# Gate and up projections as seven products of half blocks instead of eight

## The chip, the cores and the metric

The kernel runs on the 8 cores of one Trainium2 chip. Each core takes 2048 of the 16384 tokens (4 batches of 4096) and all of the weights; the cores do not talk to each other. The metric is the device time of the slowest core, in microseconds.

## What is computed

One layer of a hybrid block, of which the second half changes here:

```python
merged = (sigmoid(g_a) * y_a + sigmoid(g_p) * y_p + sigmoid(g_x) * y_x)
x = x + merged @ w_out[l]
# ---- SwiGLU channel mixer ----
h = rms_norm(x, norm_ffn[l])
x = x + (silu(h @ w_gate[l]) * (h @ w_up[l])) @ w_down[l]
return rms_norm(x, norm_final)
```

The model width is 1024 and the width of the channel mixer 2816. Matmuls take bf16 and sum in f32. The branches y_a (a short gated convolution), y_p (pooling over 2, 4, 8 and 16 positions) and y_x (attention to 256 memory tokens) come before.

## The kernel before

A core treats its tokens as two halves of 1024. Activations lie transposed, channels on partitions: `HA` holds the normed input of a half, 8 blocks of 128 channels (kc) by 1024 tokens. Weights come through a ring of 12 slots of 128 x 2048 bf16; a load reads f32 from memory, is issued from GpSimd's queue (`slot_load`, L218) and waits until the slot's readers are done and until the load eight issues back has landed. PSUM has 8 banks of 512 f32 columns, handed out in turn. All matmuls are recorded at L228. The class `Plan` writes one program for each engine: each engine runs its instructions in the order in which the Python code emits them, and a wait is set wherever an operand was written or read elsewhere.

Order of the work: mixer of half 0, merge of half 0, then `conv_units` of half 1, `merge(1, ...)` in 8 chunks of six units of 16 matmuls (`merge_chunk`: the products for gate a at L451 and L454, the pooling sums at L460 to L492, the merged block at L494), then `ffn(0)` and `ffn(1)`. `s_hook` is called at three places of each merge chunk, place 2 being in front of the last unit.

`ffn(hf)` has 22 chunks (NF) and a down stage. A chunk c has one slot with 128 columns of w_gate and 128 of w_up for all 1024 channels. `gu_g` multiplies the gate part (16 matmuls of 512 columns into two banks) and ScalarE's Silu puts it into `T[c % 2]` (L625). `gu_u` multiplies the up part, and VectorE multiplies by the Silu into `actT` (L629). Slot loads run four chunks ahead. In half 0 the first four chunks also have the output projection of half 1, two tiles of 16 matmuls each (`o1`, sum at L585), whose weights are the four `sO` slots; and in 11 of the chunks (WD) a piece of w_down is loaded (L955). The down stage has 8 tiles of 128 tokens, 44 matmuls each; per tile come the sum (L994), square (L1011), root (L325), reciprocal (L327), scaling (L331) and the store. The down stage of half 0 also norms the input tiles of half 1 and transposes them into `HA` (`Norm`, `c_trans`, by DMA on SP's queue); three of the eight norms are begun in chunks 14 to 18. `T` are seven f32 buffers of 1044 columns.

Of the kernel before, what the change touches and what calls it, by code (L numbers as in the profile page):

```python
# [85 lines left out]
def build_program():  # L86
# [36 lines left out]
    def kA(a0, n=1):  # L123
        return [("A", a) for a in range(a0, a0 + n)]
# [498 lines left out]
    def gu_g(c, s):
        u = Unit(lambda kc: rg(s, kc * P, (kc + 1) * P), s, (H0.rhs, H0.keys)).run()
        act(lambda e: e.activation(out=T[c % 2][:, 0:TM], in_=u.ps(), func=AF.Silu), u.keys(), [("T", c % 2)])  # L625

    def gu_u(c, s):
        u = Unit(lambda kc: rg(s, 1024 + kc * P, 1024 + (kc + 1) * P), s, (H0.rhs, H0.keys)).run()
        dve(lambda e: e.tensor_tensor(out=actT[:, c, :], in0=u.ps(), in1=T[c % 2][:, 0:TM], op=ALU.mult),  # L629
            u.keys() + [("T", c % 2)], kA(c))  # L630
# [229 lines left out]
    for j in range(4, 8):  # L860
# [82 lines left out]
    WD = (4, 5, 6, 8, 9, 10, 12, 13, 14, 16, 17)  # L943
    LASTB = ((0, 512), (512, 256), (768, 256))

    def ffn(hf):
        gu = [slot_load(w_gu_d[c]) for c in range(4)]
        cp, cq = [], []
        for c in range(NF):
            if c + 4 < NF:  # L950
                gu.append(slot_load(w_gu_d[c + 4]))
            if hf == 0 and c in WD:
                q = 2 * WD.index(c)
                dst = atoms(NF + q, 2)
# [12 lines left out]
        if hf == 0:
            cq.append(x1_load(1, 3))
            nxt = [3, 4]
        ydq = [x1_load(hf, 0)]  # L970
        for i in range(NT):
            b = banks(2)

            def grp(kcs, nbs=(0, 1)):
                return [(bank(b + nb), actT[:, kc, i * P:(i + 1) * P], wdT[:, kc, nb * 512:(nb + 1) * 512],
                         kc == 0, kc == NF - 1) for nb in nbs for kc in kcs]
            last = hf == 1 and i == NT - 1
            if i == 0:
# [17 lines left out]
            if hf == 0:
                for _ in range(2 if i in (2, 3) else 1):
                    if cp:
                        c_trans(*cp.pop(0))
                    if cq:  # L1000
                        q2 = cq.pop(0)
                        cp.append((Norm(T[q2][:, 0:D], [("T", q2)]).finish(), nxt[0]))
                        nxt[0] += 1
                    if nxt[1] < NT:
                        cq.append(x1_load(1, nxt[1]))
                        nxt[1] += 1
# [142 lines left out]
```

How the kernel before makes its waits and increments, by code:

```python
        def f(eng):  # L1064
            for waits, fn, semkey, inc in plan.ops[ename]:
                for sk, v in waits:
                    eng.wait_ge(sems[sk], v)
                ins = fn(eng)
                ins.then_inc(sems[semkey], inc)
```

## Time and profile before

| | us |
|---|---|
| median of 3 runs | 1153.46 |
| lowest and highest | 1153.25, 1158.1 |
| the profiled execution, its own time | 1155.09 |
| its span, slowest core (core 0) | 1153.5 |
| spans of the other cores | 1144.2 to 1151.8 |

The profile is of one execution, on the slowest core. Busy time is the time in which an engine's records run; matmuls overlap, so their mean duration (379 ns) is more than the distance between two of them. The last column of a group or of a timeline names what ended the idle time in front of an instruction. The granted clock is the share of full speed that TensorE had.

### The profile page before, as it was taken

The numbers are of one execution on the slowest core, as the hardware profiler recorded it, in microseconds if no ns is written. First come the engines' busy times: TensorE is split into PE (matmuls) and PEld (weight loads), VectorE is DVE, ScalarE is ACT, GpSimd is POOL, SyncE is SP. The second block draws the span as 40 slices with busy tenths as digits, with TensorE's granted clock in tenths as the row PEclk, the third lists the DMA queues.
The fourth block names the chain that finished last, engine by engine and source line by source line (L and its number), as shares of the span: only waits on it lengthen the run. The fifth ranks groups of instructions, "written<-read, shape, count | busy, mean of one in ns | idle before, by whom it ended". The sixth has DMA issues, their size and how long they took to land.

```text
span 1153.5 us, 14599 instructions; the slowest of 8 cores (1144.2 to 1153.5 us)
## 1 busy us (share of the span) xinstructions
PE 1117.5 (97%) x5472; PEld 543.1 (47%) x5574; DVE 475.7 (41%) x482; ACT 305.2 (26%) x490; POOL 79.0 (7%) x153
## 2 busy tenths in 40 slices
PE   7998999997999999999999999999999999999998
PEld 3665545553444444444444444444444444444444
DVE  5452555462765654654554632111324221112223
ACT  5432443423212224331212210111522121111111
POOL 1110000100011010001001000211000000000000
PEclk9998999999999999999999999999999999999999
DMA  9999861478387979345226453999966354200132
GB/s 246 173 205 203 148 128 55 80 159 127 74 137 209 258 164 175 67 123 110 56 54 110 74 146 110 204 182 171 172 164 194 101 117 82 40 1 1 37 110 110
DMA packets 78916, 146.34 MB, mean 127 GB/s; under 512 B 46571, under 2 KB 46571, under 8 KB 78592
## 3 DMA queue, kind: packets, MB, share of 16 engines
q0 software_dynamic: 21456, 77.64, 39.6%
q1 hardware_dynamic: 57392, 67.78, 20.2%
q8 instruction: 45, 0.74, 0.3%
q14 instruction: 23, 0.19, 0.1%
HBM read 185.27 MB, written 23.07 MB: 181 GB/s over the span
## 4 chain that ended last, share of the span: by engine, by line
PE 85%; DMA 10%; DVE 2%; issue 2%; ACT 1%; SPq 0%; DVEq 0%; ACTq 0%; POOLq 0%
PE ps L228 85%; DMA ring<-w_in 3%; DMA ring<-w_kv 3%; DMA arena<-hb 3%; DMA arena<-x 1%; ACT tmp L419 1%; DVE tmp L390 0%; SPq L177 0%; DVE tmp L470 0%; DVE smx L416 0%; DVE tmp L383 0%; DVE arena L397 0%; ACT tmp L387 0%; DVE tmp L483 0%; DVE hb L331 0%
## 5 line engine op out<-in xcount | busy, mean ns | idle before, releaser
L228 PE MATMUL ps<-hA,ring 128*128 128x512 bf16 (+3 forms) x2446 | 503.5, 363 | 6.6 <-ACT hA L352 2.5
L228 PEld LDWEIGHTS ps<-hA,ring 128*128 128x128 bf16 x2496 | 243.2, 98 | 259.6 <-issue 5.2
L228 PE MATMUL ps<-arena,ring 128*128 128x512 bf16 (+1 forms) x1575 | 333.3, 369 | 13.1 <-ACT tmp L460 6.1
L228 PEld LDWEIGHTS ps<-arena,ring 128*128 128x128 bf16 x1600 | 158.0, 99 | 184.2 <-issue 14.7
L228 PE MATMUL ps<-arena 128*128 128x512 bf16 (+1 forms) x838 | 180.4, 373 | 0.8
L629 DVE TENSOR_TENSOR arena<-ps,tmp 128x1024 bf16<-128x1024 f32 x44 | 53.9, 1225 | 227.9 <-PE ps L228 224.1
L228 PEld LDWEIGHTS ps<-arena 128*128 128x128 bf16 x854 | 83.6, 98 | 96.3
L625 ACT ACTIVATE tmp<-ps 128x1024 f32<-128x1024 f32 x44 | 45.0, 1023 | 253.4 <-PE ps L228 253.4
L470 DVE TENSOR_TENSOR tmp<-tmp 128x1024 f32<-128x1024 f32 (+6 forms) x40 | 49.2, 1230 | 41.4 <-ACT tmp L460 38.9
L228 PE MATMUL ps<-ring,arena 128*128 128x512 bf16 x250 | 57.4, 379 | 0.6 <-issue 0.2
L218 POOL DMA_DIRECT2D ring<-w_in x48 | 25.6, 538 | 440.0 <-PE ps L228 359.3
L994 DVE TENSOR_TENSOR tmp<-ps,tmp 128x1024 f32<-128x1024 f32 x15 | 18.4, 1224 | 79.6 <-PE ps L228 79.6
L390 DVE SCALAR_TENSOR_TENSOR tmp<-tmp,smallc 128x1024 f32<-128x1024 f32 x32 | 41.1, 1284 | 21.8 <-ACT tmp L387 20.1
L419 ACT ACTIVATE tmp<-ps,smx 128x256 f32<-128x256 f32 x64 | 30.3, 473 | 69.0 <-DVE smx L416 58.1
L454 DVE TENSOR_TENSOR tmp<-ps,tmp 128x1024 f32<-128x1024 f32 x16 | 19.6, 1224 | 64.6 <-PE ps L228 63.9
L1011 ACT ACTIVATE tmp<-tmp 128x1024 f32<-128x1024 f32 x15 | 15.8, 1056 | 114.2 <-DVE tmp L994 92.6
L218 POOL DMA_DIRECT2D ring<-w_gate_up x44 | 23.3, 531 | 324.1 <-PE ps L228 277.3
L228 PEld LDWEIGHTS ps<-ring,arena 128*128 128x128 bf16 x256 | 24.9, 98 | 30.7 <-issue 1.0
L383 DVE TENSOR_TENSOR tmp<-ps,tmp 128x1044 f32<-128x1044 f32 (+1 forms) x16 | 19.7, 1234 | 43.4 <-PE ps L228 43.4
L460 ACT ACTIVATE tmp<-ps 128x1044 f32<-128x1044 f32 (+1 forms) x16 | 16.5, 1030 | 77.2 <-PE ps L228 76.9
L451 ACT ACTIVATE tmp<-ps 128x1024 f32<-128x1024 f32 x16 | 16.4, 1024 | 76.9 <-PE ps L228 76.8
L585 DVE TENSOR_TENSOR arena<-ps,arena 128x1024 f32<-128x1024 f32 x16 | 19.6, 1222 | 38.1 <-PE ps L228 38.1
(98 smaller groups left out, 583.6 us busy)
## 6 DMA issues: line engine op xcount, KB each, us to landing
ring<-w_in POOLq DMA_DIRECT2D x48, 512.0 KB, 12.9
ring<-w_gate_up POOLq DMA_DIRECT2D x44, 512.0 KB, 12.2
arena<-x SPq DMA_DIRECT2D x32, 512.0 KB, 6.7
tmp<-x_scr SPq DMA_DIRECT2D x24, 512.0 KB, 5.3
x_scr<-arena SPq DMA_DIRECT2D x16, 512.0 KB, 3.5
out<-tmp SPq DMA_DIRECT2D x15, 512.0 KB, 3.3
arena<-w_down POOLq DMA_DIRECT2D x11, 512.0 KB, 24.3
ring<-w_kv POOLq DMA_DIRECT2D x8, 512.0 KB, 23.1
```

Source lines behind the costliest of these rows:

```text
L218: plan.op("pool", lambda e: e.dma_start(out=dst, in_=src), reads=list(reads), writes=[s.key()], dma=True)
L228: ins = e.matmul(o, l, r, start=s0, stop=s1)
L383: dve(lambda e: e.tensor_tensor(out=like(pp[:, lo:TH], u), in0=u.ps(), in1=like(ca[:, lo:TH], u), op=ALU.mult), u.keys() + [("T", tb)], [( ...
L390: dve(lambda e, k=k: e.scalar_tensor_tensor(out=cv[:, 0:TM], in0=pp[:, HALO - 2 + k:HALO - 2 + k + TM], scalar=cw(j, k), in1=cv[:, 0:TM], ...
L419: act(lambda e, h=h: e.activation(out=ex[:, h * 256:(h + 1) * 256], in_=PS[:, b * 512 + h * 256:b * 512 + (h + 1) * 256], func=AF.Exp, bia ...
L454: dve(lambda e, u=u: e.tensor_tensor(out=mm_[:, 0:TM], in0=u.ps(), in1=sa[:, 0:TM], op=ALU.mult), u.keys() + [("T", 0)], [("T", 3)])
L460: act(lambda e, u=u: e.activation(out=like(up[:, (0 if u.halo else HALO):TH], u), in_=u.ps(), func=AF.Copy), u.keys(), [("T", 4)])
L470: dve(lambda e, dst=dst, src=src, lo=lo, k=k: e.tensor_tensor(out=dst[:, lo:TH], in0=src[:, lo:TH], in1=src[:, lo - k:TH - k], op=ALU.add) ...
L585: dve(lambda e: e.tensor_tensor(out=xb(q), in0=bank(b, 2), in1=xb(q), op=ALU.add), kB(b, 2) + kX(q), kX(q))
L625: act(lambda e: e.activation(out=T[c % 2][:, 0:TM], in_=u.ps(), func=AF.Silu), u.keys(), [("T", c % 2)])
L629: dve(lambda e: e.tensor_tensor(out=actT[:, c, :], in0=u.ps(), in1=T[c % 2][:, 0:TM], op=ALU.mult), u.keys() + [("T", c % 2)], kA(c))
L994: dve(lambda e, b=b, y=y: e.tensor_tensor(out=y, in0=bank(b, 2), in1=y, op=ALU.add), kB(b, 2) + [("T", q)], [("T", q)])
```

## The change

- Gate and up of a chunk become a product of 2 x 2 blocks: rows gate and up (128 columns of weights each), inner halves channels 0 to 511 and 512 to 1023, columns tokens 0 to 511 and 512 to 1023. Strassen's scheme in Winograd's form takes seven products of half blocks, each 4 matmuls of 512 columns, for the eight of before.
- Sums of activations (`x_sums`): three new blocks held in three ring slots through the whole of `ffn`, and two blocks of `HA` overwritten by differences; 5 VectorE instructions for each of four pairs of token tiles. For half 0 they are made in merge chunks 4 and 5 of half 1, for half 1 in the down stage.
- Sums of weights (`w_sums`), one chunk ahead: one of 1024 columns on VectorE (here called W), one of 512 (A) and a difference of 1024 that rewrites the middle of the slot (S) on GpSimd. W and A go to the memory of `kT` and `vT`. S waits for W, as W reads what S overwrites; the first product of a chunk waits for S.
- Three PSUM banks a chunk; ScalarE copies four products out and does two Silus; VectorE does five sums of 512 columns in f32 and the final product, now from SBUF. `T[0]` is shared by all chunks, three more buffers alternate between even and odd chunks.
- Loads: slot c + 4 is requested behind chunk c and no longer ahead of it; the first two gate and up slots of half 0 are requested in merge chunk 6. The weight sums of chunk 0 are emitted at place 2 of merge chunk 7, and on GpSimd's queue that is ahead of the four loads of w_out.
- All eight norms of half 1 lie in the down stage of half 0, two a tile in tiles 1 to 4, in the order 0, 4, 1, 5, 2, 6, 3, 7.

```diff
     def slot_new():
+        while st["slot"] % RING in slots_held:
+            st["slot"] += 1
         s = Ref("S", st["slot"] % RING)
...
+    def x_slots():
+        for n in ("11+22", "21+22", "11+12"):
+            xq[n] = slot_new()
+            slots_held.add(xq[n].key()[1])
+
+    def x_sums(p):
+        x11, x12, x21, x22 = x_view(0, 0, p), x_view(0, 1, p), x_view(1, 0, p), x_view(1, 1, p)
+        lo, hi = [("HA", p + 1)], [("HA", p + 5)]
+
+        def dst(n):
+            return ring[:, xq[n].key()[1], :].rearrange("p (k t) -> p k t", k=4)[:, :, p * P:(p + 1) * P]
+
+        def tt(o, i0, i1, op, rd, wr):
+            dve(lambda e: e.tensor_tensor(out=o, in0=i0, in1=i1, op=op), rd, wr)
+        tt(dst("11+22"), x11, x22, ALU.add, lo + hi, [xq["11+22"].key()])
+        tt(dst("11+12"), x11, x12, ALU.add, lo, [xq["11+12"].key()])
+        tt(dst("21+22"), x21, x22, ALU.add, hi, [xq["21+22"].key()])
+        tt(x12, x12, x22, ALU.subtract, lo + hi, lo)
+        tt(x21, x21, x11, ALU.subtract, lo + hi, hi)
+
+    wx = [kT[:, :, :].rearrange("p k t -> p (k t)"), vT[:, :, :].rearrange("p k t -> p (k t)")]
+    wxk = [[("kT",)], [("vT",)]]
+
+    def w_sums(c, s):
+        e_, ek = wx[c % 2], wxk[c % 2]
+        sk = [s.key()]
+        w = rg(s, 0, SW)
+        pairs = w.rearrange("p (a b) -> p a b", a=2)
+        w11, w22 = rg(s, 0, 512), rg(s, 1536, 2048)
+        ends = w.rearrange("p (a b) -> p a b", a=4)[:, 0:4:3, :]
+        mid = rg(s, 512, 1536)
+        dve(lambda e: e.tensor_tensor(out=e_[:, 0:1024], in0=pairs[:, 0, :], in1=pairs[:, 1, :], op=ALU.add), sk, ek)
+        plan.op("pool", lambda e: e.tensor_tensor(out=e_[:, 1024:1536], in0=w11, in1=w22, op=ALU.add),
+                reads=sk, writes=[("wA", c % 2)])
+        plan.op("pool", lambda e: e.tensor_tensor(out=mid.rearrange("p (a b) -> p a b", a=2),
+                                                  in0=mid.rearrange("p (a b) -> p a b", a=2), in1=ends, op=ALU.subtract),
+                reads=sk + ek, writes=sk)
+
+    def gate_up(c, s, Q):
+        e_, ek, wa = wx[c % 2], wxk[c % 2], [("wA", c % 2)]
+        q4, q3, q1, q2 = Q
+        k4, k3, k1, k2 = [[("T", q)] for q in Q]
+        T4, T3, T1, T2 = [T[q] for q in Q]
+        lo, hi = [("HA", t) for t in range(1, 5)], [("HA", t) for t in range(5, 9)]
+        bD, bA, bC = banks(1), banks(1), banks(1)
+
...
+        L, R = slice(0, 512), slice(512, 1024)
+        prod(bD, ws_(1536), xs_("11+12"), True)
+        cp(T4[:, R], bD, [("q5", q4)] + k4)
+        prod(bA, we(1024, wa), xs_("11+22"), True)
+        cp(T3[:, L], bA, k3)
+        prod(bC, ws_(512), xh(1, 1), True)
+        cp(T4[:, L], bC, k4)
+        tt(T3[:, R], T4[:, L], T4[:, R], ALU.subtract, k4, [("qt", q3)])
+        prod(bD, ws_(1024), xh(0, 0), False)
+        cp(T1[:, L], bD, k1)
+        tt(T3[:, L], T3[:, L], T3[:, R], ALU.add, k3 + [("qt", q3)], k3)
+        prod(bA, we(512, ek), xh(0, 1), False)
+        tt(T2[:, L], bank(bA), T3[:, R], ALU.add, kB(bA, 1) + [("qt", q3)], k2)
+        prod(bC, ws_(0), xs_("21+22"), False)
+        cp(T2[:, R], bC, [("q2r", q2)], AF.Silu)
+        act(lambda e: e.activation(out=T2[:, L], in_=T2[:, L], func=AF.Silu), k2, k2)
+        tt(T3[:, L], T3[:, L], bank(bC), ALU.subtract, k3 + kB(bC, 1) + [("q2r", q2)], k3)
+        prod(bD, we(0, ek), xh(1, 0), False)
+        tt(T1[:, R], T3[:, L], bank(bD), ALU.add, k3 + kB(bD, 1), k1)
+        tt(actT[:, c, :], T1[:, 0:TM], T2[:, 0:TM], ALU.mult, k1 + k2 + [("q2r", q2)], kA(c))
 
 
...
     def s_hook(j, pos):
         s_tail()
+        if j in (4, 5) and pos == 2:
+            if j == 4:
+                x_slots()
+            x_sums(2 * (j - 4))
+            x_sums(2 * (j - 4) + 1)
+        if j == 6 and pos == 0:
+            gu0.extend(slot_load(w_gu_d[c]) for c in range(2))
+        if j == 7 and pos == 2:
+            w_sums(0, gu0[0])
 
...
     def ffn(hf):
-        gu = [slot_load(w_gu_d[c]) for c in range(4)]
-        cp, cq = [], []
+        gu = list(gu0)
+        while len(gu) < 4:
+            gu.append(slot_load(w_gu_d[len(gu)]))
+        gu0.clear()
         for c in range(NF):
-            if c + 4 < NF:
-                gu.append(slot_load(w_gu_d[c + 4]))
+            if c + 1 < NF:
+                w_sums(c + 1, gu[c + 1])
             if hf == 0 and c in WD:
                 q = 2 * WD.index(c)
                 dst = atoms(NF + q, 2)
                 plan.op("pool", lambda e, dst=dst, q=q: e.dma_start(out=dst, in_=w_down_d[:, q * D:(q + 2) * D]),
                         writes=kA(NF + q, 2), dma=True)
-            gu_g(c, gu[c])
+            r = roles[hf]
+            gate_up(c, gu[c], (r[0], r[1 + 3 * (c % 2)], r[2 + 3 * (c % 2)], r[3 + 3 * (c % 2)]))
             o1(hf, 2 * c)
-            gu_u(c, gu[c])
             o1(hf, 2 * c + 1)
-            if hf == 0 and NF - 8 <= c < NF - 5:
-                cq.append(x1_load(1, c - NF + 8))
-            if hf == 0 and NF - 6 <= c < NF - 3:
-                q = cq.pop(0)
-                n_ = Norm(T[q][:, 0:D], [("T", q)])
-                cp.append((n_.finish(), c - NF + 6))
+            if c + 4 < NF:
+                gu.append(slot_load(w_gu_d[c + 4]))
+        cq, cp, cx = [], [], []
+        ydq = [x1_load(hf, 0)]
         if hf == 0:
-            cq.append(x1_load(1, 3))
-            nxt = [3, 4]
-        ydq = [x1_load(hf, 0)]
+            cq = [(x1_load(1, t), t) for t in CO[0:2]]
         for i in range(NT):
             b = banks(2)
+            if hf == 0:
+                for p in cx:
+                    x_sums(p)
+                cx = []
+                for b_, t in cp:
+                    c_trans(b_, t)
+                    if t >= 4:
+                        cx.append(t - 4)
+                cp = []
+                if 1 <= i <= 4:
+                    for q2, t in cq:
+                        cp.append((Norm(T[q2][:, 0:D], [("T", q2)]).finish(), t))
+                    cq = [(x1_load(1, t), t) for t in CO[2 * i:2 * i + 2]]
+                if i == 1:
+                    gu0.extend(slot_load(w_gu_d[c]) for c in range(4))
+                if i == NT - 1:
+                    w_sums(0, gu0[0])
 
...
```

## Rows read from the trace of the kernel before

**Rows 1.** The page: busy us of each engine, share of the span, instructions.

```profile
PE 1117.5 (97%) x5472; PEld 543.1 (47%) x5574; DVE 475.7 (41%) x482; ACT 305.2 (26%) x490; POOL 79.0 (7%) x153
```

**Rows 2.** Busy time by stretch: from:to, length, engines, PEclk, DMA share, GB/s.

```profile
720.00:843.00 123.00, 122.42 (x560) 55.74 (x570) 26.23 (x24) 30.90 (x36) 19.01 (x36) 1.00 1.00 179
...
920.00:1071.00 151.00, 150.26 (x688) 68.41 (x700) 28.38 (x24) 25.15 (x26) 5.28 (x10) 1.00 0.24 46
```

**Rows 3.** Timeline of half 1's chunks: start, length, engine, line, operation.

```profile
982.39 1.23 DVE L629 TENSOR_TENSOR arena<-ps,tmp 128x1024 bf16<-128x1024 f32 x1 [5.68 <-PE ps L228]
...
985.76 1.02 ACT L625 ACTIVATE tmp<-ps 128x1024 f32<-128x1024 f32 x1 [5.49 <-PE ps L228]
...
996.20 1.23 DVE L629 TENSOR_TENSOR arena<-ps,tmp 128x1024 bf16<-128x1024 f32 x1 [5.68 <-PE ps L228]
```

**Rows 4.** Timeline of the last tile and of VectorE at 642: lengths and gaps.

```profile
1143.33 0.69 DVE L1022 TENSOR_TENSOR tmp<-ps,tmp 128x512 f32<-128x512 f32 x1 [0.27 <-PE ps L228]
1144.12 0.63 ACT L1025 ACTIVATE tmp<-tmp 128x512 f32<-128x512 f32 x1 [2.70 <-DVE tmp L1022]
1144.13 0.69 DVE L1029 TENSOR_TENSOR tmp<-tmp,gB 128x512 f32<-128x512 f32 x1
...
642.73 1.22 DVE L486 TENSOR_TENSOR tmp<-tmp 128x1024 f32<-128x1024 f32 x1
643.96 1.22 DVE L492 TENSOR_TENSOR tmp<-ps,tmp 128x1024 f32<-128x1024 f32 x1
```

**Rows 5.** Groups of the whole span, shapes apart: count, busy us, mean ns.

```profile
L486 DVE TENSOR_TENSOR tmp<-tmp 128x1024 f32<-128x1024 f32 x16 | 19.6, 1225 | 1.7
...
L350 DVE COPY hA<-ps 128x1024 bf16<-128x1024 bf16 x4 | 2.7, 685 | 0.9 <-PE ps L343 0.9
```

**Rows 6.** Timeline from merge chunk 7 into chunk 0 of half 0.

```profile
650.80 1.22 DVE L454 TENSOR_TENSOR tmp<-ps,tmp 128x1024 f32<-128x1024 f32 x1 [4.29 <-PE ps L228]
...
663.52 1.23 DVE L486 TENSOR_TENSOR tmp<-tmp 128x1024 f32<-128x1024 f32 x1
664.34 3.62 PE L228 MATMUL ps<-hA,ring 128*128 128x512 bf16 x16
...
665.11 0.53 POOL L218 DMA_DIRECT2D ring<-w_gate_up  x1 [2.93 <-PE ps L228]
...
671.59 1.23 DVE L585 TENSOR_TENSOR arena<-ps,arena 128x1024 f32<-128x1024 f32 x1 [4.38 <-PE ps L228]
```

**Rows 7.** Timeline from down tile 7 of half 0 into half 1.

```profile
919.89 9.44 PE L228 MATMUL ps<-hA,ring 128*128 128x512 bf16 x42
920.23 1.22 DVE L994 TENSOR_TENSOR tmp<-ps,tmp 128x1024 f32<-128x1024 f32 x1 [5.15 <-PE ps L228]
...
922.79 0.20 ACT L325 ACTIVATE stat<-stat 128x1 f32<-128x1 f32 x1
...
924.73 0.33 SPq L177 DMA_DIRECT2D out<-tmp  x1
```

**Rows 8.** Loads of w_out for half 1: first issue of 4, and landing.

```profile
606.40 0.53 POOL L218 DMA_DIRECT2D ring<-w_out  x1 [23.70 <-PE ps L228]
...
DMA to landing us min/median/max: 5.7/6.3/7.1
```

**Rows 9.** GpSimd's timeline with loads queued: first and last of 12 issues.

```profile
769.57 0.53 POOL L218 DMA_DIRECT2D ring<-w_gate_up  x1 [3.08 <-DVE arena L629]
...
802.25 0.53 POOL L218 DMA_DIRECT2D ring<-w_gate_up  x1 [2.62 <-DMA ring<-w_gate_up]
```

**Rows 10.** A wait of TensorE in merge of half 0: timeline, then PE by stretch.

```profile
287.16 5.08 PE L228 MATMUL ps<-arena,ring 128*128 128x512 bf16 x16 [6.12 <-ACT tmp L460]
...
288.00:290.00 2.00, 2.00 (x6) 0.50 0.00 0
```

**Rows 11.** VectorE's scaling in a down tile of half 0.

```profile
894.80 1.28 DVE L331 SCALAR_TENSOR_TENSOR tmp<-tmp,stat,gB 128x1024 f32<-128x1024 f32 x1
```

**Rows 12.** The page: transfers, KB each, median us from issue to landing.

```profile
out<-tmp SPq DMA_DIRECT2D x15, 512.0 KB, 3.3
```

More of the change, by code:

```diff
@@ L167, in build_program @@
     st = {"slot": 0, "pb": 0, "stat": 0, "hb": 0, "sm": 0}
-    held = set()
+    held, slots_held = set(), set()
     def act(fn, reads, writes):
@@ L621, in c_trans @@
         dma_transpose(b, HA[:, :, TOK0 + i * P:TOK0 + (i + 1) * P], [("HA", i + 1)])
[L623 to L630, printed above, removed]
+    xq = {}
@@ new lines, in x_view @@
+    def x_view(tk, kh, p):
+        t0 = TOK0 + tk * 512 + p * P
+        return HA[:, kh * 4:(kh + 1) * 4, t0:t0 + P]
+    def x_slots():
[14 more added lines that the diff above has]
+        tt(x21, x21, x11, ALU.subtract, lo + hi, hi)
@@ new lines, in gate_up, with xs_, xh, ws_ @@
+    def gate_up(c, s, Q):
[5 more added lines that the diff above has]
+        bD, bA, bC = banks(1), banks(1), banks(1)
+        def xs_(n):
+            return (lambda k: ring[:, xq[n].key()[1], k * 512:(k + 1) * 512]), [xq[n].key()]
+        def xh(tk, kh):
+            return (lambda k: HA[:, kh * 4 + k, TOK0 + tk * 512:TOK0 + (tk + 1) * 512]), (hi if tk else lo)
+        def ws_(o):
+            return (lambda k: rg(s, o + k * P, o + (k + 1) * P)), [s.key()]
+        def we(o, keys):
+            return (lambda k: e_[:, o + k * P:o + (k + 1) * P]), keys
+        def prod(b, w, x, first):
+            mms = [(bank(b), w[0](k), x[0](k), first and k == 0, k == 3) for k in range(4)]
+            def fn(e):
+                ins = None
+                for (o, l, r, s0, s1) in mms:
+                    ins = e.matmul(o, l, r, start=s0, stop=s1, skip_group_check=True)
+                return ins
+            plan.op("pe", fn, reads=w[1] + x[1], writes=kB(b, 1))
+        def cp(o, b, wr, fn=AF.Copy):
+            act(lambda e: e.activation(out=o, in_=bank(b), func=fn), kB(b, 1), wr)
+        def tt(o, i0, i1, op, rd, wr):
+            dve(lambda e: e.tensor_tensor(out=o, in0=i0, in1=i1, op=op), rd, wr)
+        L, R = slice(0, 512), slice(512, 1024)
[18 more added lines that the diff above has]
+        tt(actT[:, c, :], T1[:, 0:TM], T2[:, 0:TM], ALU.mult, k1 + k2 + [("q2r", q2)], kA(c))
@@ L871, in build_program @@
         conv_units(0, H0, j, cs[j // 2], [f0, None, (lambda k=k: s_step(H0, k + 1))])
+    gu0 = []
     def s_hook(j, pos):
         s_tail()
+        if j in (4, 5) and pos == 2:
[7 more added lines that the diff above has]
+            w_sums(0, gu0[0])
     def merge(hf, H, first):
@@ L924, in build_program @@
     TB = [2, 3, 4, 5, 6]
+    roles = [[0, 1, 2, 3, 4, 5, 6], [0, 1, 2, 3, 4, 5, 6]]
     tn = {"n": 0}
@@ L944, in build_program @@
     LASTB = ((0, 512), (512, 256), (768, 256))
+    CO = (0, 4, 1, 5, 2, 6, 3, 7)
     def ffn(hf):
-        gu = [slot_load(w_gu_d[c]) for c in range(4)]
-        cp, cq = [], []
+        gu = list(gu0)
+        while len(gu) < 4:
+            gu.append(slot_load(w_gu_d[len(gu)]))
+        gu0.clear()
         for c in range(NF):
-            if c + 4 < NF:
-                gu.append(slot_load(w_gu_d[c + 4]))
+            if c + 1 < NF:
+                w_sums(c + 1, gu[c + 1])
             if hf == 0 and c in WD:
@@ L995, in ffn @@
                 kB(b, 2) + [("T", q)], [("T", q)])
[L996 to L1006, printed above, removed]
             if i + 1 < NT:
```

## The prediction

> **What bounds the kernel now.** I read the page first, then the stretches, then single chunks of the stage that changes. TensorE is busy 97% of the span [rows 1]. By stretches, most gate and up chunks of half 0 (720 to 843 us) and those of half 1 (920 to 1071) keep it over 99% busy at a granted clock of 1.00 [rows 2]. So an instruction counts there only if it is a matmul or makes one wait. In half 1 one chunk follows another every 6.91 us: VectorE's multiplies start at 982.39 and, two chunks on, 996.20 [rows 3]. A chunk is 32 matmuls of 512 columns, so one takes 6.907/32 = 0.2158 us (the 379 ns of the records overlap). In that chunk VectorE works 1.23 us and ScalarE 1.02 us; GpSimd only issues transfers.
>
> **What is removed.** A chunk has 28 matmuls in place of 32: 6.04 us, 0.863 less. Over 44 chunks that is 38.0 us, if TensorE stays the bound.
>
> **VectorE's new work in a chunk.** Five sums of 512 f32 columns (subtract for T3 right, add for T3 left, T2 left, subtract for T3 left, T1 right) at 0.69 each [rows 4]; the product, both inputs now in SBUF, 1.225 (the SBUF-only sum of L486 costs what the PSUM one does) [rows 5]; the weight sum W of 1024 bf16 columns. For W there is no row of a bf16 pair in SBUF: the bf16 copy of 1024 columns takes 0.685, the f32 sum 1.225 [rows 5]. I take 0.69, the row with its type, and keep 1.225 for the range. Total 5 x 0.69 + 1.225 + 0.69 = 5.37. Between instructions stand 0.11 us where one needs the last one's result and about 0.02 otherwise (642.73 + 1.22 to 643.96) [rows 4]; three of the first kind and four of the second: 0.41. VectorE's round is 5.78 us of 6.04. ScalarE: four copies and two Silus of 512, each about 0.6 (half of 1.02 and some start; a 512 square is 0.63 [rows 4]), 3.6 us: no bound.
>
> **GpSimd's new work.** It gets A, a sum of 512 bf16 columns, and S, a difference of 1024. No row shows it computing: its 153 instructions are issues of 0.53 us [rows 1, 6]. Lower bound of S: VectorE's 1.225. Upper bound: the two inputs fetched one after the other, twice that, 2.45. A start of 0.16 plus 0.533 for each 512 columns fits VectorE's rows (0.69 and 1.225); with two passes but one start, S is 0.16 + 4 x 0.533 = 2.29 and A 1.23. I take these, near the upper end, as GpSimd's 0.53 for merely handing over a transfer speaks for no faster engine. The Trainium skill (GPSIMD Engine Reference, Elementwise side-by-side) has a two-input sum of 2048 columns at 4497 ns on GpSimd, so about 2.25 for 1024; by it the sum below would move by under 2 us.
>
> **The new chain.** W(c+2) stands on VectorE behind the product of chunk c; S(c+2) waits for W(c+2); all of chunk c+2 on TensorE waits for S(c+2), since S rewrites the slot. Let chunk c start at 0 and count 0.3 from the end of matmuls to the next engine (the last one starts at 919.89, VectorE at 920.23 [rows 7]). Third product ends 2.59, its copy about 3.5, T3 right can start at 3.6. The sixth ends 5.18, its Silu about 6.1; T3 left's subtraction 6.2 to 6.9, T1 right to 7.7, product 7.8 to 9.0, W to 9.7, S 9.8 to 12.1. Chunk c+2 is due at 12.08. So even with both engines free to work at once this comes out level: some 6.10 us a chunk.
>
> **Do GpSimd and VectorE work at once?** This decides the case, and the trace of before cannot say, because GpSimd never computes in it. Of VectorE's seven instructions four have both inputs in SBUF (W, T3 right, T3's addition, the product: 3.30 us), three read PSUM. Ends: nothing is lost, or S stands wholly in VectorE's round. Right behind W come T3 right and T3's addition, both with two SBUF inputs, so S, which may start when W ends, falls just on these. If they exclude each other the round is 5.78 + 2.29 = 8.07; A, which comes behind S and a 0.53 issue, then falls on the PSUM readers and costs nothing. I take this end: a sum of two SBUF tensors is the one kind of work both would do, and no row supports counting on overlap. The Trainium skill (SBUF — State Buffer, Who interferes with whom) says that the two engines share one SBUF port pair, held by whichever comes first for its whole instruction, also against a VectorE instruction with two SBUF inputs if GpSimd reads SBUF. By that rule the chunk is the 8.07; without it 6.10. It speaks against this change.
>
> In chunks 0 to 3 of half 0 the output projection adds two tiles of 16 matmuls, 6.91 us, and only 2 x 1.23 to VectorE [rows 6]: TensorE, at 12.95, stays the bound over 8.07 + 2.46 = 10.5 there. These give 4 x 0.863 = 3.5 back. Of the other 40, about 39.5 are paced by VectorE (one starts from an idle engine): 39.5 x (8.07 - 6.907) = 45.9 lost.
>
> **Entry to half 0.** W(0) stands in VectorE's queue behind all pool sums of merge chunk 7: L486 ends at 664.75 [rows 6], W(0) near 665.5, S(0) from 665.6 to 667.9. TensorE would start chunk 0 at 664.34 and now starts at 668.0: 3.6 lost. Behind S(0) on GpSimd stand the four w_out loads, which before went out from 606.40 on [rows 8]; nothing hides that move. Each landed after 5.7 to 7.1 us, median 6.3 [rows 8]; when loads are queued one comes through about every 3.0 us (12 issues, 11 steps, between 769.57 and 802.25, most of them held for an earlier load [rows 9]). The last lands at 668.0 + 6.3 + 3 x 3.0 = 683.3. The first output tile is due at 668.0 + 6.04 = 674.0: 9.3 lost, bounds 3 and 12. Behind a stall of 6.1 us at 281 to 287 the granted clock was 0.50 (1.2 GHz) and 16 matmuls took 5.08 instead of 3.45 us [rows 10]: 1.6 more. The two early gate_up loads and the three held slots cost nothing: merge chunk 7's slots come free one merge chunk before they are used.
>
> **Sums of activations.** 20 VectorE instructions of 512 bf16 columns a half, 0.43 to 0.69 each. In merge chunks 4 and 5, 10 each, under 7 us: of six units of 3.45 us VectorE idles 4.29 us in one stretch alone [rows 6] and PSUM holds three further units. In the down stage VectorE does a sum, a short reciprocal and a scaling a tile now, 1.22 + 1.28 and some 0.2 [rows 7, 11]; two norms (2.9) and five sums (at most 3.5) make 9.0 of 9.5 us, and the last sums are a tile ahead. The moved norms leave the chunks, where VectorE has no room. The four SP transfers more a tile fit in 9.5 us. Cost 0; if one came late, chunk 0 of half 1 would wait for it.
>
> **Entry to half 1.** Down tile 7's square and root hold ScalarE until 3.1 us behind the end of the matmuls (919.89 to 922.99 [rows 7]); the copy that frees the first bank then ends at 3.7, 1.2 late. The fourth product's copy goes to buffer 2, which holds tile 7's output: store issued at 924.73, landing 3.3 later [rows 7, 12], so 8.1 behind the matmuls; the copy and TensorE's seventh product follow at 9.1 in place of 5.2: 3.9 lost. At the end of each half the last product is 3 to 6 us behind TensorE; the first down tile has 40 matmuls, 8.6 us, before it: 0.
>
> **Sum.** 1153.5 - 3.5 + 45.9 + 3.6 + 9.3 + 1.6 + 3.9 = 1214.3 of span. The profiled execution took 1155.1 with a span of 1153.5; the median of the three runs is 1153.46, so I carry the +60.8 over to it: 1214.
>
> **Rivals.**
> (1) The engines overlap freely. A chunk is 6.10: 44 x (6.91 - 6.10) = 35.5 gained, 18.4 lost at the two entries: 1136. It decides wherever S does not hold VectorE back; the change wins if S and T3 right run at once. For it: three of seven instructions read PSUM, and nothing in the trace shows a collision. If W takes 1.225 besides, VectorE's round is 6.32: 44 x 0.59 = 25.8 gained, 18.4 lost, 1146, at the edge of what can be told from no change.
> (2) They exclude each other, but VectorE wins the short gap before T3's addition, and S runs beside the PSUM readers. The sums that exclude each other make 3.30 + 2.29 + 1.23 = 6.8, with handovers 7.0: 1153.5 + 39.5 x 0.1 - 3.5 + 18.4 = 1172. Against it: S has waited since the end of W and the gap is 0.11 us.
> (3) The 2 us for which TensorE waits in each chunk bring the clock to 1.2 GHz, or S costs above 2.45: beyond 1240. Against it: before, the clock was down only behind waits of 6 us [rows 10].
> (4) The change doesn't do what it says, 32 matmuls' worth of time remains: excluded by the count of products, 7 x 4.
>
> **How the numbers follow.** Forecast 0.45 (1196 to 1240: S at 1.7 to 2.45, W up to 1.225, entries of 10 to 21). Rival 1 0.24 with W fast, 0.06 with W slow (half of that faster, half the same). Rival 2 and what lies between it and the forecast 0.15. Rival 3 0.07. What I have not seen, on the fast side, 0.03. Both signs hold much, so the range reaches from rival 1's 1136 less 6 for cheaper entries to the forecast's upper end: 1130 to 1240; the forecast alone is 1196 to 1240. A measurement of this kernel tells 0.5%, 5.8 us, from no change. Faster 0.24 + 0.03 + 0.03 = 0.30, same 0.03, slower 0.45 + 0.15 + 0.07 = 0.67.
>
> **What would show it.** The forecast: chunks spaced near 8.1 us, VectorE over 70% busy with gaps or long instructions where S runs, TensorE waiting for GpSimd's difference. Rival 1: chunks near 6.1, S beside T3 right with neither longer. Entries: TensorE idle 3.6 us at 664, then 9 us before the first output tile with ring<-w_out as releaser, and near 4 us in chunk 0 of half 1 behind ScalarE's copy. I am wrong above all if S neither lengthens nor delays its neighbours on VectorE.

## The result, and the profile after

| | before | after |
|---|---|---|
| median of 4 runs | 1155.78 us | 1178.57 us |
| ratio, with its 95% interval | 1 | 1.0191 [1.015, 1.0231] |
| the profiled execution | 1155.09 us | 1176.2 us |
| its span, slowest core | 1153.5 us (core 0) | 1174.7 us (core 6) |
| spans of all cores | 1144.2 to 1153.5 | 1163.6 to 1174.7 |

The change makes the kernel 1.9% slower. Slower was the likelier side of the forecast, but by 61 us; it is 23. In some executions, whatever the kernel, the cores of one die run at a lower granted clock and take longer (one of the four after, 1251.77 us); the two medians of the table hold such executions, the ratios and all later times do not. The page of the kernel after, its first section, and its waits between 660 and 1100 us (who waited for whom: us in total, times, longest):

```profile
PE 1104.1 (94%) x5398; PEld 526.3 (45%) x5398; DVE 732.5 (62%) x786; ACT 402.7 (34%) x704; POOL 235.8 (20%) x241
```

```profile
PE ps L696 <- POOL ring L666: 37.0, 37, 3.3
...
PE ps L230 <- DMA ring<-w_out: 9.1, 1, 9.1
...
PE ps L696 <- ACT tmp L701: 4.5, 3, 2.2
```

Against [rows 1] VectorE (DVE) has 257 us more and GpSimd (POOL) 157; TensorE waits 37 times for S, GpSimd's difference at L666, 1 us each on average. (Of the matmuls of before some records are missing, 5472 against 5574 weight loads; the weight loads, now 5398, are fewer by the full 176, four a chunk.) The groups of the chunks, shapes apart, between 700 and 1100 us:

```profile
L704 DVE TENSOR_TENSOR tmp<-tmp 128x512 f32<-128x512 f32 x84 | 127.3, 1515 | 7.7 <-ACT tmp L701 3.4
...
L666 POOL TENSOR_TENSOR ring<-ring 128x1024 bf16<-128x1024 bf16 x41 | 97.4, 2375 | 205.6 <-DVE kT L663 135.8 <-DVE vT L663 69.8
...
L704 DVE TENSOR_TENSOR tmp<-tmp,ps 128x512 f32<-128x512 f32 x84 | 57.1, 680 | 8.6 <-DVE tmp L704 4.5 <-PE ps L696 2.6
```

Two kinds of VectorE sum of the same shape stand here. Those with one input in PSUM take 680 ns, as in [rows 4]. Those with both in SBUF, the on-chip memory that holds the slots, the activations and `T` (they are T3 right and T3's addition, from here on the pair), take 1515 on average, and the timeline of half 1 shows which:

```profile
996.85 1.23 DVE L704 TENSOR_TENSOR arena<-tmp 128x1024 bf16<-128x1024 f32 x1
...
997.99 0.68 DVE L663 TENSOR_TENSOR vT<-ring 128x1024 bf16<-128x1024 bf16 x1
...
998.59 3.21 DVE L704 TENSOR_TENSOR tmp<-tmp 128x512 f32<-128x512 f32 x2
...
998.88 2.38 POOL L666 TENSOR_TENSOR ring<-ring 128x1024 bf16<-128x1024 bf16 x1 [3.04 <-DVE vT L663]
...
1001.40 1.02 PE L696 MATMUL ps<-ring 128*128 128x512 bf16 x4 [0.91 <-POOL ring L666]
1001.72 0.68 DVE L704 TENSOR_TENSOR tmp<-ps,tmp 128x512 f32<-128x512 f32 x1
1001.79 1.17 POOL L664 TENSOR_TENSOR kT<-ring 128x512 bf16<-128x512 bf16 x1
```

Behind W (L663) the pair takes 3.21 us; S runs at the same time and ends at 1001.26, and only then does the pair end, at 1001.80. In the last chunk of half 1, where no S follows, the same pair takes 1.48:

```profile
1090.41 1.48 DVE L704 TENSOR_TENSOR tmp<-tmp 128x512 f32<-128x512 f32 x2
1091.81 0.68 DVE L704 TENSOR_TENSOR tmp<-ps,tmp 128x512 f32<-128x512 f32 x1
```

The products of chunks 0 and 20 of half 1 start at 946.97 and 1089.27: 7.115 us a chunk, where [rows 3] give 6.907 and 28 matmuls need 6.04. One round of VectorE, from start to start in the rows above and their neighbours, is 3.13 (pair) + 0.60 + 0.84 + 0.80 (the three that read PSUM) + 1.14 (product) + 0.60 (W) = 7.11: the round fills the chunk.

**Where the 21 us of span come from**, by TensorE's first matmul of each stage:

| stage | before | after | difference |
|---|---|---|---|
| merge ends, half 1 | 664.34 | 658.4 | -5.9 (another core) |
| chunks 0 to 3 of half 0 | 55.3 | 69.3 | +14.0 |
| chunks 4 to 21 of half 0 | 124.3 | 128.0 | +3.7 |
| down, half 0 | 76.0 | 78.9 | +2.9 (granted clock 0.96) |
| chunks of half 1 | 151.95 | 158.1 | +6.1 |
| down, half 1, to the end | 81.7 | 81.95 | +0.3 |

So the larger part comes from the entry to half 0 and not from the steady chunks. The first row is no gain: core 0 of before came late to this point (its cores 1 to 3 at 655 to 656), cores 0 to 3 of after come to it at 654 to 657. The 2.9 of the down stage are the clock of cores 4 to 7 alone: on cores 0, 1 and 3 of the same execution, with the same norms in it and a clock of 1.00, the stage takes 76.0 as before.

That entry, in the timeline, answers to [rows 6]:

```profile
658.54 0.69 DVE L663 TENSOR_TENSOR kT<-ring 128x1024 bf16<-128x1024 bf16 x1
...
659.14 1.22 DVE L494 TENSOR_TENSOR tmp<-ps,tmp 128x1024 f32<-128x1024 f32 x1
659.37 2.12 POOL L666 TENSOR_TENSOR ring<-ring 128x1024 bf16<-128x1024 bf16 x1 [41.46 <-DVE kT L663]
660.46 2.11 DVE L496 TENSOR_TENSOR arena<-tmp 128x1024 bf16<-128x1024 f32 x1
661.43 2.16 POOL L220 DMA_DIRECT2D ring<-w_out  x4
661.75 1.27 PE L696 MATMUL ps<-ring 128*128 128x512 bf16 x4 [3.35 <-POOL ring L666]
...
678.77 9.07 PE L230 MATMUL ps<-ring,arena 128*128 128x512 bf16 x32 [9.13 <-DMA ring<-w_out]
```

TensorE waits 3.35 us for S(0) and 9.13 for w_out, whose loads GpSimd issues only behind S(0), at 661.43 and so some 55 us later than before [rows 8]. After that the two output tiles take 8.91 us, from 678.77 to the next product at 687.68, instead of 6.91, with the clock down (TensorE's clock is the column before the last two):

```profile
662.00:669.00 7.00, 7.00 (x26) 0.76 0.69 109
669.00:679.00 10.00, 0.87 (x4) 0.68 1.02 154
679.00:688.00 9.00, 9.00 (x34) 0.79 0.99 207
688.00:700.00 12.00, 12.00 (x52) 0.90 0.71 178
```

On this core the mean clock stayed at 1.00 only from 700 us on. The waits explain only a part of that. Core 1 of the same execution waited as long (3.35 and 9.82 us) and had its full clock back by 688:

```profile
679.00:688.00 9.00, 9.00 (x33) 0.76 0.86 182
688.00:700.00 12.00, 12.00 (x57) 1.00 0.72 197
```

So had cores 0, 2 and 3. Cores 4 to 7 had 1.00 from 685 to 690 and then 0.81 to 0.84 from 690 to 696, with TensorE busy all the time.

The entry also shows one S beside both kinds of instruction. L494 of the kernel after, with one input in PSUM, runs beside S(0) and takes 1.22 us. L496, with two in SBUF, starts before S(0) ends at 661.49 and takes 2.11; in the kernel before the same instruction stands at L494 and took 1.23:

```profile
665.98 1.23 DVE L494 TENSOR_TENSOR arena<-tmp 128x1024 bf16<-128x1024 f32 x1
```

### The profile page after: what moved, and what is told of

Read it like the earlier page. It is cut to its first block, busy times and chain, and to the rows that moved or that the text cites. A ratio compares the mean times of both kernels' runs of the same rounds, so it can differ in the third digit from the quotient of the medians.

```text
span 1174.7 us, 15935 instructions; the slowest of 8 cores (1163.6 to 1174.7 us)
## 1 busy us (share of the span) xinstructions
PE 1104.1 (94%) x5398; PEld 526.3 (45%) x5398; DVE 732.5 (62%) x786; ACT 402.7 (34%) x704; POOL 235.8 (20%) x241
## 4 chain that ended last, share of the span: by engine, by line
PE 72%; DMA 9%; POOL 7%; DVE 4%; issue 3%; ACT 3%; SPq 0%; POOLq 0%; ACTq 0%; DVEq 0%
PE ps L230 61%; PE ps L696 11%; POOL ring L666 7%; DMA ring<-w_in 3%; DMA ring<-w_q_t 2%; ACT tmp L701 2%; DMA arena<-x 1%; DMA ring<-w_out 1%; DMA ring<-w_kv 1%; DVE kT L663 1%; DVE vT L663 1%; ACT tmp L421 1%; DVE tmp L392 0%; SPq L177 0%; DVE smx L418 0%
## 5 line engine op out<-in xcount | busy, mean ns | idle before, releaser
L230 PE MATMUL ps<-hA,ring 128*128 128x512 bf16 (+4 forms) x1088 | 205.4, 347 | 5.6 <-ACT hA L354 2.6
L701 ACT ACTIVATE tmp<-ps 128x512 f32<-128x512 f32 x220 | 126.2, 592 | 117.6 <-PE ps L696 104.8
L666 POOL TENSOR_TENSOR ring<-ring 128x1024 bf16<-128x1024 bf16 x44 | 103.7, 2358 | 253.9 <-DVE kT L663 183.9
L230 PEld LDWEIGHTS ps<-hA,ring 128*128 128x128 bf16 x1088 | 106.5, 98 | 98.2 <-issue 13.7
L704 DVE TENSOR_TENSOR tmp<-tmp 128x512 f32<-128x512 f32 x88 | 132.6, 1507 | 13.3 <-ACT tmp L701 8.7
L696 PE MATMUL ps<-ring 128*128 128x512 bf16 x352 | 90.7, 380 | 37.0 <-POOL ring L666 37.0
L696 PE MATMUL ps<-hA,ring 128*128 128x512 bf16 x352 | 84.4, 382 | 2.3 <-ACT tmp L701 2.3
L696 PEld LDWEIGHTS ps<-ring 128*128 128x128 bf16 x352 | 31.8, 97 | 87.2 <-issue 54.8
L704 DVE TENSOR_TENSOR tmp<-tmp,ps 128x512 f32<-128x512 f32 x88 | 59.9, 680 | 9.6 <-DVE tmp L704 4.7
L704 DVE TENSOR_TENSOR arena<-tmp 128x1024 bf16<-128x1024 f32 x44 | 54.4, 1237 | 5.7 <-DVE tmp L704 2.8
L1117 DVE TENSOR_TENSOR tmp<-ps,tmp 128x1024 f32<-128x1024 f32 x15 | 18.4, 1224 | 59.5 <-PE ps L230 59.5
L696 PEld LDWEIGHTS ps<-hA,ring 128*128 128x128 bf16 x352 | 34.6, 99 | 45.2 <-issue 5.1
```

The costliest lines, as they stand in the source:

```text
L230: ins = e.matmul(o, l, r, start=s0, stop=s1)
L666: plan.op("pool", lambda e: e.tensor_tensor(out=mid.rearrange("p (a b) -> p a b", a=2), in0=mid.rearrange("p (a b) -> p a b", a=2), in1=en ...
L696: ins = e.matmul(o, l, r, start=s0, stop=s1, skip_group_check=True)
L701: act(lambda e: e.activation(out=o, in_=bank(b), func=fn), kB(b, 1), wr)
L704: dve(lambda e: e.tensor_tensor(out=o, in0=i0, in1=i1, op=op), rd, wr)
```

## The experiments

The theory to test: S on GpSimd and a VectorE instruction with both inputs in SBUF exclude each other. The rivals: VectorE is simply full (load), or TensorE waits at the end of the chain W, S, first product (latency). Chunk spacings are those of the products in chunks 4 to 20 of half 0, or of as many as the text says.

**All sums on VectorE.** In `w_sums`:

```diff
-        plan.op("pool", lambda e: e.tensor_tensor(out=e_[:, 1024:1536], ...   # A
+        plan.op("dve", lambda e: e.tensor_tensor(out=e_[:, 1024:1536], ...
-        plan.op("pool", lambda e: e.tensor_tensor(out=mid..., op=ALU.subtract), ...   # S
+        plan.op("dve", lambda e: e.tensor_tensor(out=mid..., op=ALU.subtract), ...
```

> A and S, the weight sums of GpSimd, go to VectorE; everything else as in the changed kernel. Exclusion theory (in the changed kernel S and VectorE's instructions with two SBUF inputs take turns; of the 7.11 us of a chunk 5.38 are VectorE's own and 1.73 the turns): VectorE's round becomes 5.38 + 0.35 (A) + 0.60 (S) = 6.33 us, T3's addition takes 0.69 again instead of 2.4, the chunk is 6.3; and as no sum stands on GpSimd's queue ahead of the w_out loads, their wait of 9 us goes. 1178.6 - 39.5 x 0.78 - 13 = about 1135. Load theory (VectorE is simply full, its long sums are long by themselves): two more instructions make the chunk 7.11 + 0.95 = 8.06, about 1200. Latency theory (the chain W, S, TensorE bounds): S at 0.6 instead of 2.1 shortens the chain, the chunk falls to 6.04, about 1123.

Measured: 1132.2 us, ratio to before 0.9793 [0.9713, 0.9874], the span of the profiled execution 1130.6. The chunk is 6.54 us (718.04 to 822.61, 16 steps). More work on VectorE made it faster: the load theory is out. The latency theory wanted 6.04, but a full VectorE could hide that here, so it is tested separately below. The pair is back at 1.48 and S takes 0.69:

```profile
981.69 0.69 DVE L666 TENSOR_TENSOR ring<-ring 128x1024 bf16<-128x1024 bf16 x1
...
982.30 1.48 DVE L704 TENSOR_TENSOR tmp<-tmp 128x512 f32<-128x512 f32 x2
```

The chunk is 0.2 above the 6.33 expected: W, A and S take 0.60, 0.52 and 0.61 from start to start, 1.73 together where I had counted 1.55.

**A and S left out.**

```diff
-        plan.op("pool", ...)   # A and S, both
-        prod(bA, we(1024, wa), xs_("11+22"), True)
+        prod(bA, we(512, ek), xs_("11+22"), True)
```

> A and S are left out (two of the seven products use wrong weights), all waits on them with them; W and the rest stay. Exclusion theory: VectorE's round is its own 5.38, TensorE bounds with 28 matmuls, chunk 6.04, 1178.6 - 39.5 x 1.07 - 13 = about 1123. Load theory: the chunk stays near 7.1 and the time near 1165. Latency theory: 6.04, as exclusion. The pair of 512-column f32 sums behind W takes 1.4 and not 3.2 us by the exclusion and latency theories.

Measured: 1114.3 us (one run), chunk 6.04 (715.92 to 812.54, 16 steps), the pair 1.48. The load theory falls here again; exclusion and latency are not told apart.

**Nobody waits for S.**

```diff
-        plan.op("pool", ... out=mid..., in0=mid..., in1=ends, op=ALU.subtract), reads=sk + ek, writes=sk)
+        plan.op("pool", ... out=hb[3]..., in0=mid..., in1=ends, op=ALU.subtract), reads=sk + ek, writes=[("hb", 3)])
```

> S runs on GpSimd at the same moment with the same inputs, behind W, but writes to a spare buffer: no instruction of TensorE waits for it (the half blocks that S should make stay as loaded, so two products have wrong weights). Exclusion theory: VectorE is held up as before, the chunk stays 7.1 though nobody waits for S, and S stays 2.4 long; the time changes only by the 3.4 us wait of chunk 0: about 1175. Latency theory: with TensorE free of S the chunk is 6.04 to 6.1, about 1135.

Measured: 1170.33 us (one run), chunk 7.13 (735.49 to 849.58, 16 steps).

```profile
985.28 3.21 DVE L704 TENSOR_TENSOR tmp<-tmp 128x512 f32<-128x512 f32 x2
985.51 2.44 POOL L666 TENSOR_TENSOR hb<-ring 128x1024 bf16<-128x1024 bf16 x1 [2.90 <-DVE kT L663]
```

TensorE now waits for nothing of S. In the chunks it waits for copies (37.6 us in 39 waits): ScalarE's Silu waits for a sum of VectorE (97.0 us in 41 waits), and the copies stand behind it in ScalarE's queue. The chunk is as long as in the kernel after. The wait for w_out is still there and longer, 14.7 us, as chunk 0 now starts at once (655.88) while the loads still go out behind S (659.16). The latency theory is out: S costs by standing in VectorE's way, not by its own length in the chain.

**S beside the PSUM readers.** W and S two chunks ahead with a third buffer, emitted behind T3's addition; A on VectorE; the entries mended as in the next but one:

```diff
+            if c % 3 == 2: return hb[3][:, a:b] if b <= 1024 else hb[2][:, a - 1024:b - 1024]
...
         tt(T3[:, L], T3[:, L], T3[:, R], ALU.add, k3 + [("qt", q3)], k3)
+        if nxt is not None:
+            w_sums(c + 2, nxt)
```

> With both entries mended, S stays on GpSimd with its full 2.1 us, but W and S are made two chunks ahead (third buffer in hb) and emitted behind T3's addition, so S runs beside T2 left, T3 left's subtraction and T1 right, which read PSUM; A goes to VectorE. Exclusion theory: none of the three gets longer than 0.69, S stays near 2.12 and VectorE's round is 5.38 + 0.35 = 5.73: chunk 6.04 to 6.15, about 1112. Rival (it is GpSimd's sum as such that slows VectorE): the three PSUM readers get longer by some 1.7 us together and the chunk stays near 7.1 to 7.4, about 1155.

Measured: 1114.5 us, ratio to before 0.9694 [0.964, 0.9747]. The chunk is 6.00 (726.25 to 822.26, 16 steps, chunks 5 to 21), in which VectorE makes up a delay; TensorE's chunks 4 to 21 take 6.05 each (711.67 to 820.66).

```profile
990.40 1.33 DVE L712 TENSOR_TENSOR arena<-tmp 128x1024 bf16<-128x1024 f32 x1
...
993.33 0.68 DVE L671 TENSOR_TENSOR hb<-ring 128x1024 bf16<-128x1024 bf16 x1
...
993.93 0.42 DVE L672 TENSOR_TENSOR hb<-ring 128x512 bf16<-128x512 bf16 x1
994.27 0.68 DVE L712 TENSOR_TENSOR tmp<-ps,tmp 128x512 f32<-128x512 f32 x1
994.51 2.12 POOL L674 TENSOR_TENSOR ring<-ring 128x1024 bf16<-128x1024 bf16 x1 [3.33 <-DVE hb L672]
...
994.87 1.47 DVE L712 TENSOR_TENSOR tmp<-tmp,ps 128x512 f32<-128x512 f32 x2
```

S still takes its 2.12 us on GpSimd, in the same kernel and every chunk, but beside instructions that read PSUM; none of them gets longer (0.68, and 1.47 for two), and S is 2.12 instead of 2.38. Where S's end still meets the product, which has two SBUF inputs, the product takes up to 1.33 instead of 1.23 (the row at 990.40; the S of that chunk runs from 988.52 to 990.64). This carries the verdict: it is not GpSimd's sum as such, it is what VectorE reads meanwhile. With all sums made it is the fastest kernel of the case, 3.1% faster than before, though 3.15 us of the wait for w_out are left in it.

**A copy, and a memset, in the place of S.** Both from the kernel in which nobody waits for S:

```diff
-        plan.op("pool", lambda e: e.tensor_tensor(out=hb[3]..., in0=mid..., in1=ends, op=ALU.subtract), ...
+        plan.op("pool", lambda e: e.tensor_copy(out=hb[3][:, :], in_=mid), ...      # the one
+        plan.op("pool", lambda e: e.memset(hb[3][:, :], 0.5), ...                   # the other
```

> As the kernel in which nobody waits for S, but S is a copy of 1024 columns with one input instead of a difference with two (its result goes to a spare buffer, the half blocks S should make stay as loaded). Exclusion theory: a copy reads SBUF too, so T3's addition waits for it; if it takes half of S, 1.1 us, the pair T3 right and T3's addition takes about 3.2 - 1.0 = 2.2 and the chunk is 7.11 - 1.0 = 6.1, about 1135. Rival (only a second input of GpSimd collides): the pair takes 1.48, chunk 6.04.

> As before, but S is a memset of 1024 columns, which reads nothing (the half blocks S should make stay as loaded). If only reads of SBUF exclude each other, the pair T3 right and T3's addition takes 1.48 us whatever the memset's length, and the chunk is 6.04. If any use of SBUF by GpSimd excludes VectorE's instructions with two SBUF inputs, the pair is longer by the memset's length less some 0.4.

Measured: 1132.48 us and 1129.85 us for the profiled executions (spans 1130.9 and 1128.2), chunks 6.13 and 6.05. The copy, then the memset:

```profile
999.00 2.12 DVE L703 TENSOR_TENSOR tmp<-tmp 128x512 f32<-128x512 f32 x2
999.28 1.30 POOL L666 COPY hb<-ring 128x1024 bf16<-128x1024 bf16 x1 [3.02 <-DVE kT L663]
```

```profile
995.50 1.48 DVE L702 TENSOR_TENSOR tmp<-tmp 128x512 f32<-128x512 f32 x2
995.71 0.95 POOL L666 MEMSET hb<- 128x1024 bf16 x1 [3.34 <-DVE kT L663]
```

A copy of 1.30 us lengthens the pair by 0.64. With S the pair ended 0.54 us behind S; the same rule gives the copy exactly this: 0.28 (its start) + 1.30 + 0.54 - 1.48 = 0.64. For the memset, started 0.21 into the pair, it would give 0.22; measured is nothing, and of the 36 sums of this kind between 940 and 1080 us none takes over 0.693. So one input of GpSimd is enough to collide, and a write alone does not, at least not with this instruction. The chunk times decide nothing here: with the copy VectorE's round is 6.03, already TensorE's own 6.04, and one chunk of 7.41 among the 16 steps makes the mean 6.13.

**The entries alone.**

```diff
-        if j == 7 and pos == 2:
+        if j == 7 and pos == 0:
             w_sums(0, gu0[0])
+        if j == 7 and pos == 2:
+            sO_.extend(slot_load(w_out_d[q]) for q in range(4))
...
-    roles = [[0, 1, 2, 3, 4, 5, 6], [0, 1, 2, 3, 4, 5, 6]]
+    roles = [[0, 1, 2, 3, 4, 5, 6], [0, 4, 6, 5, 1, 2, 3]]
```

> Only the two entries are mended: the weight sums of chunk 0 go to the start of merge chunk 7, the four w_out loads are requested in merge chunk 7 behind them, and in half 1 even chunks use buffers 4, 6, 5 and odd ones 1, 2, 3. If the entries cost what the trace says (TensorE waits 3.4, 9.1 and 2.2 us, and about 3 us by the lower clock behind them), 1178.6 - 17 = about 1161 with chunks unchanged at 7.11. Rival: the time lost there is made up elsewhere (VectorE, not TensorE, is late), then under 5 us are gained.

Measured: 1157.3 us (1152.85 and 1161.69), ratio to before 1.001 [0.9913, 1.0108], where the kernel after had 1.019. In the profiled executions cores 0 to 3 span 1147.5 to 1150.1, against 1163.6 to 1169.9 in the kernel after, about 18 less. Neither the wait for w_out nor that for S(0) is left; TensorE waits only 33.2 us for S in 37 pieces of at most 1.2, and 2.3 us for copies. The chunk is 7.10 as in the kernel after. The entries cost some 18 us, apart from what the chunks cost; nearly all of it lies at half 0, as at half 1 the waits for copies go from 3.15 to 0.91.

**Only A on GpSimd**, behind T3's addition, S on VectorE, entries mended:

```diff
-        tt(T3[:, L], T3[:, L], T3[:, R], ALU.add, k3 + [("qt", q3)], k3)
+        tt(T3[:, L], T3[:, L], T3[:, R], ALU.add, k3 + [("qt", q3)], k3 + [("gate",)])
+        if nxt is not None:
+            a_sum(c + 1, nxt)      # on GpSimd, reads ("gate",)
```

> With both entries mended, S moves to VectorE (0.60 us start to start) and only A (1.17 us) stays on GpSimd, now released by T3's addition of the chunk ahead, so that it runs beside the three VectorE instructions that read PSUM. Exclusion theory: A meets no instruction with two SBUF inputs for more than its first tenth, VectorE's round is 5.38 + 0.60 = 5.98, TensorE bounds: chunk 6.04 to 6.15, time 40 x 1.0 below the kernel with mended entries (1150 to 1160), so about 1112, 3.5% faster than the kernel before. Rival (any GpSimd sum beside VectorE costs its length, whatever VectorE reads): 5.98 + 1.17 = 7.15, about 1155.

Measured: 1122.6 us, ratio to before 0.9791 [0.9721, 0.9861]: neither the 1112 nor the rival's 1155. The chunk is 6.33 (722.62 to 817.54, 15 steps).

```profile
992.19 0.69 DVE L672 TENSOR_TENSOR ring<-ring 128x1024 bf16<-128x1024 bf16 x1
992.80 0.68 DVE L710 TENSOR_TENSOR tmp<-tmp 128x512 f32<-128x512 f32 x1
...
993.66 0.69 DVE L710 TENSOR_TENSOR tmp<-tmp 128x512 f32<-128x512 f32 x1 [0.17 <-DVE tmp L710]
...
994.63 1.14 POOL L658 TENSOR_TENSOR vT<-ring 128x512 bf16<-128x512 bf16 x1 [4.72 <-DVE tmp L710]
...
994.87 1.47 DVE L710 TENSOR_TENSOR tmp<-tmp,ps 128x512 f32<-128x512 f32 x2
...
995.92 1.02 PE L702 MATMUL ps<-ring,vT 128*128 128x512 bf16 x4 [0.18 <-POOL vT L658]
```

A lengthens nothing, as the theory says. But the round was counted too tight: S waits for W (W starts at 991.40, S at 992.19, 0.79 instead of 0.60), and T3's addition often starts 0.86 behind T3 right instead of 0.80. With such waits the round is about 6.2 and not 5.98; and TensorE waits 19 times for A, 6.1 us in all. What makes up the rest to 6.33 is not shown.

## Why the prediction came out as it did

**Direction and mechanism held.** The forecast took the end at which GpSimd's difference and VectorE's instructions with two SBUF inputs exclude each other. The trace of after, the kernel in which nobody waits for S and the one with S beside the PSUM readers bear it out. The Trainium skill (SBUF — State Buffer, Who interferes with whom) says that a VectorE instruction with two SBUF inputs contends with a GpSimd instruction that reads SBUF, and not with one that only writes it. The traces agree on both counts: the pair went from 1.48 to 3.21 us beside S and stayed at 1.48 beside the memset. Rival 1 (free overlap) did not occur; its whole chain with free overlap was never run, the nearest to it is the memset in the place of S, with a chunk of 6.05. Rival 2 did not occur: from chunk 1 on S falls on the pair and never on the PSUM readers; only S(0) of half 0 ran beside one. Rival 3 did not either, the granted clock was 1.00 in the chunks from 700 us on, with TensorE waiting about 1 us in each, and S took 2.38, not over 2.45.

**The step that failed is the size of VectorE's round**, the 8.07 us of "Do GpSimd and VectorE work at once?". It is 7.11, and both of its terms were too high.
- Its own part: 5.78 forecast. Without S the rows give 1.40 (pair) + 0.60 + 0.84 + 0.80 + 1.14 + 0.60 = 5.38. I had added gaps to durations; but independent instructions overlap, 0.68 us long and 0.60 apart. The row 642.73 to 643.96 in [rows 4] showed a gap near zero, and behind [rows 6] stands even an overlap (L486 ends at 664.75, its follower starts at 664.66 in the same trace); a round has to be summed from start to start.
- The part of S: 2.29 forecast, 7.11 - 5.38 = 1.73 measured. S alone takes 2.12 (2.29 from the model of two passes was not bad; A's 1.23 is 1.17 beside the PSUM readers), and the collision makes it 2.38. But S starts 0.29 into T3 right's 0.68, so 0.39 of it lies beside T3 right; and T3's addition ends 0.54 behind S, where from T3 right's end it needs 0.80, another 0.26. 2.38 - 0.39 - 0.26 = 1.73. I had put all of S into the round.
- 0.40 + 0.56 = 0.96 us, 39.5 times: 38 us. The forecast for the chunks was +45.9; measured are +3.7 in half 0 and 6.1 less the entry's 3.15 in half 1, +6.7. That is the whole miss, 61 against 23. A round near the 6.91 of before turns an error of 0.96 us in a round of 7.11 into a factor of nearly seven in the time it costs; the range of the forecast case (1196 to 1240) should have reached down for that, as the row with overlap stood in the trace.

**That all else came out right is partly luck.** Without the chunks paced by VectorE the forecast has 14.9 us (entries 18.4 less 3.5), the stages above have 14.5. But in these 14.5 stand -5.9 for a late core of before and +2.9 for the clock of the down stage, neither of which the change makes, and the clock at the entry to half 0 cost about three times what was forecast.

**Entry to half 0**: 3.6 and 9.3 forecast, 3.35 and 9.13 measured. The first is 3.35 on every core; the second runs from 5.7 to 10.8 over the eight, so that it is hit to 0.2 is luck. The lower clock behind it was put at 1.6; the stage is 14.0 longer with 3.5 gained and 12.5 of waits, so it was about 5. By the same sum it was 3.3 to 4.5 on cores 0 to 3, whose clock was back at 1.00 by 688: two waits cost more than the 1.6 behind the one of [rows 10], and the rest on core 6 is the fall to 0.81 at 690, which follows no wait of this core.

**Entry to half 1**: 3.9 forecast. TensorE waits 0.98 and 2.17 for ScalarE's copies, the second held for the store from that buffer (3.35 us on the transfer out<-tmp), together 3.15 (2.9 on the seven other cores). The two mechanisms were the ones named.

```profile
938.39 1.02 PE L696 MATMUL ps<-hA,ring 128*128 128x512 bf16 x4 [0.98 <-ACT tmp L701]
...
942.57 0.60 ACT L701 ACTIVATE tmp<-ps 128x512 f32<-128x512 f32 x1 [3.35 <-DMA out<-tmp]
...
943.31 1.02 PE L696 MATMUL ps<-hA,kT 128*128 128x512 bf16 x4 [2.17 <-ACT tmp L701]
```

**W** takes 0.68 us (0.69 forecast, the row with its type), a sum of 512 bf16 columns 418 to 422 ns. The one W that ran beside an A took 1.68:

```profile
729.08 1.16 POOL L664 TENSOR_TENSOR vT<-ring 128x512 bf16<-128x512 bf16 x1
729.13 1.68 DVE L663 TENSOR_TENSOR vT<-ring 128x1024 bf16<-128x1024 bf16 x1
```

The sums of activations and the moved norms cost nothing in their place, as forecast: on the cores with a clock of 1.00 the down stage of half 0 takes 76.0 us before and after.

**Chances.** The case that came true (exclusion, S in the round) had 0.45, with a range that missed it by 17 us; the time lay in what was called rival 2 and what lies between it and the forecast, 0.15, for another reason than rival 2's.

## What to carry to other kernels

Before work goes to GpSimd, write down for each of its instructions which VectorE instruction it will run beside. In these kernels one with both inputs in SBUF was held up by a GpSimd sum or copy, one that reads PSUM was not. With the entries mended, S beside the pair left the kernel level with the one before (1.001), S beside the PSUM readers (and A on VectorE) made it 3.1% faster. And where a new bound lies close to the old one, take rounds from start to start in the trace: 0.40 us too much for gaps and 0.56 too much for S were here the difference between 61 and 23 us. Look also at what a compute instruction on a queue of transfers holds back: one sum ahead of four loads, itself waiting for VectorE, cost a wait of 9 us.

## What the runs showed of the hardware that I had not expected

- GpSimd's bf16 sums: 2.12 us for 1024 columns and 1.14 to 1.17 for 512 undisturbed; copy 1.30 (beside the pair), memset 0.95 for 1024 columns. A memset of GpSimd and a VectorE sum of two SBUF inputs ran side by side without loss; a copy did not.
- VectorE's instructions without a dependency overlap in their records by 0.08 us (0.68 long, 0.60 apart), so busy time overstates what it is bound by: the parts of one 7.11 us round add up to 7.2 us of records.
- When the two collide, both pay: S 2.12 to 2.38, the pair 1.48 to 3.21 us.
- After waits of 3.35 us and, 8 us later, 6.8 to 9.8 us, cores 0 to 3 were back at a granted clock of 1.00 by 688 us. Cores 4 to 7 came back too and then fell to 0.81 to 0.84 from 690 to 696 without a wait, and ran the down stage of half 0 at 0.96 to 0.98. Why they did is open.
